# Six rounds of the tensor engine's expert-up stage written out instead of looped

## What is computed

```python
def block(args):
    xc, ec, gc = args                      # tokens, chosen experts, gates
    u = jnp.take(expert_down, ec, axis=0)
    hdn = jax.nn.gelu(jnp.einsum('ted,td->te', u, xc))
    vsel = jnp.take(expert_up, ec, axis=0)
    return jnp.einsum('te,ted->td', gc * hdn, vsel)
```

## Time and profile before

| what | value |
|---|---|
| median of the timed runs | 3018.91 us |
| the profiled execution, its own time | 3036.75 us |
| span of that execution, first to last instruction | 3034.7 us |
| TensorE matmul busy | 2999.1 us (99%) |
| TensorE weight load busy | 2676.0 us (88%) |
| VectorE, ScalarE, GpSimd busy | 65%, 49%, 31% |
| share of the chain that ended last spent on TensorE | 95% |
| mean granted clock of TensorE | 0.994 |
| rounds 0 to 6 of the up stage | 1268.0 to 1828.3 us |

### The profile page before, as it was taken

The page is one execution under the profiler, slowest core; times in us unless marked ns, Lnnn a source line. Parts: engine busy times, 40 slices in busy tenths (PEclk is TensorE's granted clock), DMA queues, the critical chain, the costliest instruction groups (busy, mean ns, idle before and its releaser), DMA issues.

```text
span 3034.7 us, 44598 instructions
## 1 busy us (share of the span) xinstructions
PE 2999.1 (99%) x16703; PEld 2676.0 (88%) x16703; DVE 1970.3 (65%) x2549; ACT 1473.1 (49%) x1794; POOL 945.9 (31%) x675
## 2 busy tenths in 40 slices
PE   9999999999999999999999999999999999999998
PEld 8999888888888888998999999999878888888887
DVE  5445564688875555687988976645776555555554
ACT  6445454555564444544444444554555434444443
POOL 3110000088888887155777840000000000000000
PEclk9999999999999999999999999999999999999999
DMA  7764467577777778898999985654446666666664
GB/s 228 246 205 140 147 216 253 187 210 204 213 204 203 225 209 260 296 334 308 351 363 351 349 308 193 191 180 136 132 146 187 192 191 193 191 191 193 190 193 153
DMA packets 227280, 672.30 MB, mean 222 GB/s; under 512 B 57116, under 2 KB 60838, under 8 KB 226737
## 3 DMA queue, kind: packets, MB, share of 16 engines
q1 hardware_dynamic: 157696, 549.79, 55.5%
q0 software_dynamic: 63680, 103.36, 11.8%
q10 hardware_dynamic: 5744, 16.99, 1.5%
HBM read 631.85 MB, written 38.12 MB: 221 GB/s over the span
## 4 chain that ended last, share of the span: by engine, by line
PE 95%; DVE 2%; issue 1%; ACT 1%; DMA 1%; ACTq 0%; SPq 0%; DVEq 0%
PE ps L1954 14%; PE ps L2248 10%; PE ps L2095 8%; PE ps L2097 8%; PE ps L2096 8%; PE ps L1933 8%; PE ps L1934 8%; PE ps L1932 8%; PE ps L1953 7%; PE ps L2247 5%; PE ps L1950 1%; PE ps L2261 1%; PE ps L2260 1%; PE ps L2262 1%; DVE w_lo L691 1%
## 5 line engine op out<-in xcount | busy, mean ns | idle before, releaser
L691 DVE TENSOR_TENSOR w_lo<-raw,w_hi 128x1024 fp32r<-128x1024 f32 (+2 forms) x1072 | 1274.0, 1194 | 855.7 <-ACT w_hi L686 801.1
L686 ACT ACTIVATE w_hi<-raw 128x1024 fp32r<-128x1024 f32 (+2 forms) x1072 | 1107.4, 1034 | 1274.0 <-PE ps L1934 338.4
L1954 PE MATMUL ps<-x_all,w_hi 128*128 128x512 f32 x1920 | 667.7, 390 | 0.0
L1953 PE MATMUL ps<-x_all,w_lo 128*128 128x256 f32 x1920 | 541.7, 282 | 2.3 <-DVE w_lo L691 2.3
L551 POOL DMA_INDIRECT gates<-srch x256 | 486.4, 1900 | 160.5 <-issue 78.5
L2248 PE MATMUL ps<-acts,w_hi 128*128 128x416 f32 x1680 | 514.4, 370 | 3.7 <-issue 3.7
L2247 PE MATMUL ps<-acts,w_lo 128*128 128x208 f32 x1680 | 437.7, 261 | 5.3 <-issue 4.9
L2095 PE MATMUL ps<-w_hi,x_all 128*128 128x440 f32 (+2 forms) x1152 | 436.4, 379 | 0.4 <-DVE w_lo L691 0.4
L1954 PEld LDWEIGHTS ps<-x_all,w_hi 128*128 128x128 f32 x1920 | 360.5, 188 | 74.6
L2096 PE MATMUL ps<-w_lo,x_all 128*128 128x440 f32 (+2 forms) x1152 | 424.7, 369 | 0.0
L2097 PE MATMUL ps<-w_hi,x_all 128*128 128x440 f32 (+2 forms) x1152 | 424.7, 369 | 0.0
(11 more groups left out here) (390 smaller groups left out, 3522.4 us busy)
## 6 DMA issues: line engine op xcount, KB each, us to landing
raw<-in_peer_down SPq DMA_DIRECT2D x256, 512.0 KB
raw<-in_peer_up SPq DMA_DIRECT2D x256, 512.0 KB
raw<-in_w_mlp_in SPq DMA_DIRECT2D x128, 512.0 KB
raw<-in_w_mlp_out SPq DMA_DIRECT2D x128, 512.0 KB
raw<-in_w_in SPq DMA_DIRECT2D x112, 440.0 KB
raw<-in_w_in SPq DMA_DIRECT2D x96, 428.0 KB
raw<-in_w_out SPq DMA_DIRECT2D x64, 512.0 KB
gates<-zero POOLq DMA_DIRECT2D x32, 512.0 KB, 4.9
```

The costliest lines, as they stand in the source:

```text
L686: act.activation(w_hi[:, c % RING, 0:2 * n], raw[:, c % RING, 0:2 * n], ACT.Copy).then_inc(hi_made, 1)
L691: nc.vector.tensor_tensor(w_lo[:, c % RING, 0:2 * n], raw[:, c % RING, 0:2 * n], w_hi[:, c % RING, 0:2 * n].bitcast(F32), ALU.subtract).th ...
L1953: mm(o[:, 0], wl, xh, start=False, stop=False)
L1954: last = mm(o, wh, both, start=False, stop=(k == KT - 1))
```

## The change

TensorE's rounds 0 to 6 of the up stage are written out, where round 0 was written out and rounds 1 to 6 were one loop. The other engines' programs are untouched, and so are all matmuls, their order and the counts that they wait for.

```diff
@@ -2307,8 +2307,7 @@
             down(TURNED, beside(FROM * SUB))
             with pe.Fori(TURNED + 1, PEER_ROUNDS) as r:
                 down(r)
-            up(0)
-            with pe.Fori(1, PEER_ROUNDS - 1) as r:
+            for r in range(PEER_ROUNDS - 1):
                 up(r)
```

## The result

The changed kernel takes 3027.38 us (median of 19 runs, 3018.39 to 3035.57) against 3019.12 for the kernel before (19 runs, 3015.61 to 3024.1). The ratio is 1.0024, with a 95% interval of 1.0017 to 1.0032. Timed again later beside other kernels it came out at 1.0028 (1.0016 to 1.0039). So the change makes the kernel slower by 7 to 8 us (5 to 10 by the interval), where 1 us was forecast.

A forecast was written before the change was run, and what follows sets the result against it. TensorE, busy 99% of the span, was taken as the bound. 3018.9 + 0 (back edges) + 0 (own code) + 1.0 (weight stream) + 0 (MLP edge) = 3019.9 us, range 3015 to 3025.5.

The forecast's parts named there:

- What bounds the kernel: Whole kernel: TensorE, busy 99% of the span; clean up rounds take 77.2 us, looped or written out.
- the pauses: Up rounds 1 and 6 of the first profile: 19.4 us together over 77.2 a round, inferred hardly present in timed runs.
- Part 1, the back edges: Up loop's seam: five taken branches removed, 1.05 us of sequencer time, hidden by a 2.6 us lead, so worth 0.
- The rival with a fetched branch: Up loop's seam: each back edge fetches its target, 3.71 us against 2.6 cover; 5.6 us faster, 3013.3 us; chance 5%.
- Part 2(a), late code: Written-out up rounds: TensorE may wait for about 20 new instruction packets; priced at 0, as round 0 takes 77.2 us.
- Part 2(b), time taken from the weight stream: Up rounds 2 to 6: 20 instruction packets delay weight slices; bounds 0 and 19.4 us, taken as +1.0 us.
- one exposure of 0.97: Up rounds 2 to 6: one instruction packet delaying a weight slice enough to hold TensorE, up to 0.97 us.
- the slower rival: Up rounds 2 to 6: fetches hit a saturated weight stream, up to 0.97 us per packet, 3038.3 us; chance 6%.
- its point of decision: Up rounds 2 to 6: the saturated-stream rival decides from seven exposures on, 6.8 us or 0.2%.
- the ring's lead: Up stage's weight loads: a ring of four slices was said to take up delays before they reach TensorE.
- Part 2(c), what comes later: MLP loop's branch behind the up stage: 3.71 us, just covered; taken as 0, uncovered 3.7 us, 3023.6 us, chance 4%.
- a shift that it doesn't see: No place named: an unforeseen shift of the time, no size given; chance 2%.

The follow-up runs named there:

- experiment 1: Against the kernel before: TensorE's up rounds 1 to 6 in a loop of two passes with three rounds in the body; 3031.14 us, ratio 1.0046.
- experiment 4: Up-stage weight loads halved, in the kernel before (loop) and in the changed kernel (written out): 3016.68 and 3016.44 us, ratios 0.9991 and 0.9994 against the kernel before.
- the half: Against the kernel before: TensorE's up rounds 0 to 3 written out, rounds 4 to 6 in a loop; 3022.56 us, ratio 1.0022.

## Why the prediction was wrong

**What bounds the kernel: right in kind, wrong in the slack.** That a looped and a written-out round have the same length of 77.2 us is right: rounds 0 and 1, written out, have it in every profile of the changed kernel, and looped rounds 4 and 5 in the second profile of the kernel before. But I read the clean rounds of the first profile as the state of the timed runs. There TensorE waited 0.3 us for `w_lo` in 340 us; in the second profile of the same kernel it waited 1.3 us, and the rounds lost 2.8. My own argument had said that the pauses are not in the timed runs. I took their 19.4 us off the sum, but not their effect on the rounds behind them.

**Part 1, the back edges: right.** With the weight stream lightened, the kernels with and without the loop are 0.24 us apart, with every round at 77.2 us in both profiles, so the five branches had no price that can be measured. The rival with a fetched branch doesn't apply to this body, but is real for a long one (experiment 1: 5.78 us, of which 3.4 showed).

**Part 2(a), late code: right, within 1 us.** The code is longer by 20 packets, and no wait of a matmul in the stage lacks a known cause; 0.8 us of the weight loads' waits do, in two of the three profiles.

**Part 2(b), time taken from the weight stream: the step that failed.** I bounded it at 0 and 19.4 us and took one exposure of 0.97, allowing three. The runs put it at about 7 us, the 7 to 8 of the whole less the 0.7 at the output. The prediction's own sign of this came true, for it said that it is wrong if clean rounds come out at 78.5 us or more with waits for `w_lo`, and rounds 2 to 6 took 78.6 to 82.2 in the first profile (in the other two, three and two of the five are over 78.5). The mechanism's place is shown: the loss is in rounds 2 to 6, at waits for `w_lo`, with the packets, and it vanishes when the stream is lightened (experiment 4). Per packet, if all the time is put down to the packets, it is 0.0024 x 3019 / 20 = 0.36 us for the change, 0.0022 x 3018 / 12 = 0.55 for the half, and 0.48 for the three-round body. The outcome is the slower rival, "the fetches hit a saturated weight stream", just past its point of decision; it had 6%. The error in weighing was to count how often the stream had reached TensorE (once) and not how near it was. Of the ring's lead nothing stands in the waits until it is used up. The size of one delay was about right, some 0.5 us measured on a slice within a bound of 0.97. What was wrong is how many reach TensorE: one was taken, and 0.36 us a packet against some 0.5 us a slice means, as an estimate, that most of the delay does. The argument against the rival, that round 0 bears the same packets, was true and did not carry over: round 1 bears them as well, at a share of 0.96, and the next rounds don't.

**Why a packet costs that much stays open.** I priced it by bytes and by engine time, and copies of data do not confirm either: 20 pieces of the same size cost nothing measurable, 80 cost 0.15% in either queue, and nine packets of SyncE's instructions cost nothing. A q8 packet takes longer, some 1.0 us for 0.61, but not enough for that, since 80 data pieces are still 49 us of engine time against 20. Something more about TensorE's instruction packets, such as the DMA engine that serves them, seems to be needed. The trace doesn't name engines, and no run here settles it.

**Part 2(c), what comes later: the MLP edge did not move, the output did.** In the changed kernel its branch took 4.57 us, and TensorE paused 0.73 us:

```profile
2662.45 0.39 PE L1934 MATMUL ps<-w_hi,a_lo 128*128 128x512 f32 x1
2663.57 0.49 PE L1950 MATMUL ps<-x_all,w_hi 128*128 128x512 f32 x1 [0.73 <-issue]
```

The step is 1.12 us, where it was 0.26. But in the thirteen profiles with the loop as it was it ranges from 0.26 to 1.45, 0.95 on average, and in the five with all rounds written out from 0.70 to 1.12, 0.82 on average. So the change did nothing here that can be seen, and the 0.26 that the prediction read was the lowest of the thirteen: that the branch is just covered was the luck of one profile. What did come later is the 0.7 us at the output, which the prediction had only as a shift that it doesn't see.

**One long wait passes by another way.** The longest wait of the changed kernel, 3.2 us in round 6, is not a late slice alone. The timeline of the other engines there:

```profile
1778.96 1.06 ACT L686 ACTIVATE w_hi<-raw 128x1024 fp32r<-128x1024 f32 x1 [1.50 <-DMA raw<-in_peer_up]
...
1782.23 0.16 DVE L1505 TENSOR_TENSOR big<-big 128x1 f32<-128x1 f32 x1 [5.88 <-DMA big<-hid_rows,big]
1782.31 1.22 DVE L691 TENSOR_TENSOR w_lo<-raw,w_hi 128x1024 fp32r<-128x1024 f32 x1
```

`w_hi` of the slice was ready by 1780.0, but VectorE stood 5.88 us at line 1505 for a gather, and `w_lo`, behind it in program order, began at 1782.3, 2.3 us later. The prediction had looked at the loads of weights only. The gathers' queue q0 takes 35% of the 16 engines' time beside the 59% of the weights, and VectorE turns a late gather into a late weight slice.

## What to carry to other kernels

Before you write out a loop, look at the instruction queue: if the body stays at the engine (no packets over its passes) and the seam shows no step, there is nothing to gain at the seam, and every 16 KB of new code is one more transfer beside those of the data. Judge the room for it from a profile whose time is that of the timed runs. Where one has pauses, take a second one: what comes after a pause may be flattered by it. And read a step that is "just covered" from more than one profile.

In a stage like this one, with the DMA share at 0.95 to 0.99, waits for data that are rare don't mean that they are far. An experiment that lightens the stream shows in two runs whether a cost passes through it.

## What the runs showed of the hardware that was not expected

- 20 packets of TensorE's instructions (0.33 MB, 0.24% of what the queues moved) cost 0.18 to 0.28% of the whole kernel in three measurements, in rounds with a DMA share of 0.88 to 0.98, and nothing at 0.77. 20 data packets of the same size cost nothing measurable (0.02%, at most 0.11%), 80 of them 0.15%.
- From the issue of the first of the last eight output copies to the end it is 7.3 us in all thirteen profiles with the loop as it was, 7.7 and 7.9 with the three-round body and with half of the rounds written out, and 7.9 to 8.0 with all of them, though the copies are the same.
- A TensorE loop of 1063 instructions (four 16 KB packets) ran five back edges with no fetch and 0.21 us a branch. With three rounds in the body the one back edge took 5.78 us, and the MLP's took 3.61 to 4.83 over all twenty profiles. The Trainium skill (Advanced Engine Details and Errata, section Control Flow Timing) gives a compare-and-branch as about 108 ns. The branches here that stayed at the engine took 208 ns at the median and 76 ns at the least, so for a taken one the trace doesn't bear that figure out.
- A contiguous 16 KB copy, written as one row, was carried out as 16 packets of 1 KB; two rows of 16 KB that don't adjoin stayed two packets.
